# Short output tiles' weights split in own memory, first weights loaded first, and a norm factor moved to a later stage

## The reference, cut to what matters

```python
h = h + mix                                  # mix ends in a product with w_o, 1024 x 1024
hn = rmsnorm(h, norm_ffn[layer])             # (h * rsqrt(mean(h*h) + eps)) * gain
u, gate = jnp.split(hn @ w_in, 2, axis=-1)   # each 2816 wide: 22 tiles of 128
a = conv_b + sum(ext[:, j:j + T] * conv_w[j] for j in range(CONV_W))
h = h + (jax.nn.silu(a) * gate) @ w_out
```

## Time and profile before

| | |
|---|---|
| median of 3 runs | 1583.49 us (1582.51 to 1584.4) |
| the profiled execution, its own time | 1583.71 us |
| its span in the trace | 1582.2 us |
| PE busy | 1535.4 us (97%) |
| DVE, ACT, POOL busy | 977.3, 748.6, 464.3 us |

### The profile page before, as it was taken

One profiled execution on the slowest core, in us unless ns is written; L12 is line 12 of the kernel. 1 busy time (PEld: TensorE's weight loads), 2 busy tenths in 40 slices (PEclk: granted clock), 3 DMA queues, 4 the chain that ended last, 5 costly groups with the idle time before them and its releaser, 6 DMA issues. The chain is left out here.

```text
span 1582.2 us, 36661 instructions
## 1 busy us (share of the span) xinstructions
PE 1535.4 (97%) x13694; PEld 1456.7 (92%) x13694; DVE 977.3 (62%) x1700; ACT 748.6 (47%) x1283; POOL 464.3 (29%) x495
## 2 busy tenths in 40 slices
PE   7999999998999999999999999999999999999997
PEld 7999999988989999999999999755899899999997
DVE  5767666756977777633354444678559776776221
ACT  6444444425456566522244455666444565565110
POOL 1222222213765565101000100223137655551000
PEclk9999999999999999999999999999999999999999
DMA  6222222212232322222333434599422223223230
GB/s 211 69 83 90 90 83 76 77 54 102 81 92 96 103 82 88 93 77 83 91 115 114 138 100 148 182 342 356 139 81 81 90 98 101 85 87 103 91 107 25
DMA packets 52883, 174.14 MB, mean 110 GB/s; under 512 B 7266, under 2 KB 9330, under 8 KB 52770
## 3 DMA queue, kind: packets, MB, share of 16 engines
q1 hardware_dynamic: 47858, 155.46, 30.2%
q0 software_dynamic: 4912, 17.12, 3.0%
HBM read 159.99 MB, written 12.57 MB: 109 GB/s over the span
## 5 line engine op out<-in xcount | busy, mean ns | idle before, releaser
L533 ACT ACTIVATE w_hi<-w_raw 128x1024 fp32r<-128x1024 f32 (+2 forms) x146 | 148.0, 1014 | 299.7 <-PE acc L2025 267.0
L1033 DVE TENSOR_TENSOR w_lo<-w_raw,w_hi 128x1024 fp32r<-128x1024 f32 (+2 forms) x144 | 180.9, 1257 | 141.8 <-ACT w_hi L533 138.9
L2025 PE MATMUL acc<-xl,w_hi 128*128 128x288 f32 x1008 | 228.1, 308 | 14.9 <-DVE w_lo L1238 9.4
L2025 PE MATMUL acc<-xh,w_hi 128*128 128x288 f32 x1008 | 216.7, 297 | 0.0
L2025 PE MATMUL acc<-xh,w_lo 128*128 128x288 f32 x1008 | 216.7, 297 | 0.0
L2025 PEld LDWEIGHTS acc<-xl,w_hi 128*128 128x128 f32 x1008 | 162.8, 190 | 23.0 <-DVE w_lo L1238 9.4
L2217 PE MATMUL aux<-ffn_xsl,w_hi 128*128 128x288 f32 x576 | 169.9, 295 | 3.1 <-issue 2.9
L2217 PE MATMUL aux<-ffn_xsh,w_lo 128*128 128x288 f32 x576 | 170.1, 295 | 0.0
L2217 PE MATMUL aux<-ffn_xsh,w_hi 128*128 128x288 f32 x576 | 169.9, 295 | 0.0
L2025 PEld LDWEIGHTS acc<-xh,w_hi 128*128 128x128 f32 x1008 | 163.1, 190 | 0.0
L2025 PEld LDWEIGHTS acc<-xh,w_lo 128*128 128x128 f32 x1008 | 162.7, 190 | 0.0
(11 more groups left out here) (341 smaller groups left out, 3456.2 us busy)
## 6 DMA issues: line engine op xcount, KB each, us to landing
w_raw<-w_fi_in SPq DMA_DIRECT2D x88, 512.0 KB, 3.7
w_raw<-w_fo_in SPq DMA_DIRECT2D x32, 512.0 KB, 3.6
att_Vd<-cache_v_in SPq DMA_DIRECT2D x32, 512.0 KB, 5.6
w_raw<-w_mix_in SPq DMA_DIRECT2D x31, 512.0 KB, 3.7
w_raw<-w_kv_in SPq DMA_DIRECT2D x16, 512.0 KB, 3.7
w_raw<-w_qg_in SPq DMA_DIRECT2D x16, 512.0 KB, 3.6
dec_Kd<-cache_k_in SPq DMA_DIRECT2D x16, 512.0 KB, 6.7
w_raw<-cache_k_in SPq DMA_DIRECT2D x16, 512.0 KB, 6.9
```

The lines of the kernel that those rows point to most:

```text
L533: nc.scalar.activation((w_hi[:, pos.slot % SPL] if dst is None else dst)[:, 0:width], w_raw[:, pos.slot, 0:width] if raw is None else raw[ ...
L1033: nc.vector.tensor_tensor(low[:, 0:width], w_raw[:, pos.slot, 0:width] if raw is None else raw[:], high[:, 0:width].bitcast(F32), ALU.subt ...
L2025: mm = nc.tensor.matmul(dst[:, hf, 0:HALF], W[:, 128 * (j0 + j):128 * (j0 + j) + 128], x[:, HALF * hf:HALF * hf + HALF], start=(first and ...
```

## The change

- Start: the first half of the first weight block is loaded and split first, then come the gains and the first tile of x; `S0` waits for the last tile of x.
- Output tiles of layer 0: the four short blocks 40 to 43 each get a quarter of `own_hi` and `own_lo`. They are split during tiles 1 and 2, block 44 in tile 2, block 45 after tile 7. `xh` is made ahead of the square (both layers), and from tile 4 on DVE makes the `xl` of a tile after the `add_h` of the next.
- Plain pairs: `sil` is no longer multiplied by `rms`. POOL multiplies `g0` by `rms` instead, in the first four fast pairs, behind its other work there; only `g_hi` at the end waits for it. In pair 3 the low parts of xn come ahead of the weight sums, and these ahead of the convolution's taps.

The core of the diff (renames and declarations left out):

```diff
@@ SP, start
+            sp.dma_start(w_raw[:, 0, 0:512], d["w_mix"][0][:, 0:512]).then_inc(w_half, 16)
+            sp.dma_start(gains[:], d["gains"]).then_inc(ld_table, 16)
             sp.dma_start(h[:, 0, :], d["x"][0]).then_inc(ld_h[0], 16)
-            sp.dma_start(gains[:], d["gains"]).then_inc(ld_table, 16)
...
-            sp.dma_start(w_raw[:, 0, 0:512], d["w_mix"][0][:, 0:512]).then_inc(w_half, 16)
@@ ACT, out_tile and start
-                square(n_s, m)
                 if g is not None:
                     gain_hi(xh, m, g)
+                square(n_s, m)
...
+            act.wait_ge(w_half, 16)
+            nc.scalar.activation(w_hi[:, 0, 0:512], w_raw[:, 0, 0:512], ACT.Copy).then_inc(s_hi, 1)
             act.wait_ge(setup, 1)
@@ ACT, ffn, loop over m
-                    elif m == AHEAD:
-                        hi(Pos(B_REST + 2), W_REST, ready=(block_done, B_WO0 + AHEAD + 1), dst=own_hi)
-                    elif m == AHEAD + 1:
-                        hi(Pos(B_REST + 3), W_REST)
-                        hi(Pos(b_in), ready=(block_done, B_REST + 1))
-                    elif m and m != DT - 2:
-                        hi(Pos(b_in - 8 + m + 2), W_REST if 2 <= m < AHEAD else 1024)
+                    elif m == 0:
+                        hi(Pos(B_REST - 1))
+                    elif m < 3:
+                        for r in (2 * m - 2, 2 * m - 1):
+                            hi(Pos(B_REST + r), W_REST, ready=(block_done, B_WO0 + AHEAD + 1), dst=rest_hi[r])
+                    if layer == 0 and m == 2:
+                        hi(Pos(b_in), ready=(block_done, B_REST - 1))
                     out_tile(m, n_h0 + m + 1, None, s_base + m, G_FFN + 8 * layer)
+                if layer == 0:
+                    hi(Pos(b_in + 1), ready=(block_done, B_REST))
@@ DVE, ffn, loop over m (the lo calls move as the hi calls do)
+                    if layer == 0 and m == AHEAD:
+                        continue
+                    if layer == 0 and m > AHEAD:
+                        gain_lo(xl, xh, m - 1, G_FFN + 8 * layer, x_base + m - 1)
+                        continue
                     gain_lo(xl, xh, m, G_FFN + 8 * layer, x_base + m)
+                if layer == 0:
+                    gain_lo(xl, xh, DT - 1, G_FFN + 8 * layer, x_base + DT - 1)
+                    lo(Pos(b_in + 1))
@@ DVE, plain_pair
-                    taps(k, f)
                     if f == PLAIN - 1:
+                        x_lo_raw(f)
                         weight_sum(0, 0, PLAIN // 2)
                         weight_sum(1, 0, PLAIN // 2)
-                    x_lo_parts(f)
+                        taps(k, f)
+                    else:
+                        taps(k, f)
+                        x_lo_raw(f)
+                    x_lo_sums(f)
                     if f < PLAIN - 1:
                         lo(Pos(b_in + 2 * k + 3, i, 4))
-                    dve.wait_ge(silr_ok, PLAIN * layer + f + 1)
+                    dve.wait_ge(sil_ok, n + 1)
@@ POOL, start, plain_pair, and the end of fast_pair
+            pool.wait_ge(ld_h[DT - 1], 16)
             pool.dma_start(S0[:].rearrange("p n v -> p (n v)"), d["s0"][0]).then_inc(s0_in, 16)
...
-                    pool.wait_ge(sil_ok, n + 1)
-                    nc.gpsimd.tensor_tensor(sil[:], sil[:], rms[:], ALU.mult).then_inc(silr_ok, 1)
...
+                    if isinstance(i, int) and f < 2 * PLAIN:
+                        pool.wait_ge(prod_ok, FT * layer + f - PLAIN + 1)
+                        nc.gpsimd.tensor_tensor(g0[:, f - PLAIN], g0[:, f - PLAIN], rms[:], ALU.mult).then_inc(g_rms, 1)
@@ ACT, g_hi
+                    if f < PLAIN:
+                        act.wait_ge(g_rms, PLAIN * layer + f + 1)
@@ PE, short tiles
-                             split=(own_hi, own_lo) if own else None)
+                             split=(rest_hi[m - AHEAD], rest_lo[m - AHEAD]))
```

More of the change, by code:

```diff
@@ L151, in build @@
         own_hi, own_lo = own_slot("hi", [P, 1024], F32R), own_slot("lo", [P, 1024], F32R)
+        rest_hi, rest_lo = [[t[:, W_REST * r:W_REST * (r + 1)] for r in range(AHEAD)] for t in (own_hi, own_lo)]
         kd0 = fr
@@ L312, in build @@
         s0_in, s0_mul, s1_ps, s1_ok, s1_out, s_out = [sem(n) for n in ("s0_in", "s0_mul", "s1_ps", "s1_ok", "s1_out", "s_out")]
-        st_in, ubuf_ok, u_ok, c0_ok, c2_ok, sil_ok, silr_ok, prod_ok, gh_ok, glo_ok, cst_ok = [sem(n) for n in (
-            "st_in", "ubuf_ok", "u_ok", "c0_ok", "c2_ok", "sil_ok", "silr_ok", "prod_ok", "gh_ok", "glo_ok", "cst_ok")]
+        st_in, ubuf_ok, u_ok, c0_ok, c2_ok, sil_ok, g_rms, prod_ok, gh_ok, glo_ok, cst_ok = [sem(n) for n in (
+            "st_in", "ubuf_ok", "u_ok", "c0_ok", "c2_ok", "sil_ok", "g_rms", "prod_ok", "gh_ok", "glo_ok", "cst_ok")]
         out_cst = sem("out_cst")
@@ L652, in _ @@
                 gain_hi(xh, m, G_MIX)
-                if m == 0:
-                    act.wait_ge(w_half, 16)
-                    nc.scalar.activation(w_hi[:, 0, 0:512], w_raw[:, 0, 0:512], ACT.Copy).then_inc(s_hi, 1)
                 if m == 1:
@@ L1248, in add_square @@
                     nc.vector.tensor_tensor(ssq[:], ssq[:], (rms, sq)[m % 2][:], ALU.add).then_inc(ssq_done, 1)
+            half_lo(0, s_hi, 1, s_lo)
             for m in range(DT):
                 gain_lo(xl, xh, m, G_MIX, m)
-                if m == 0:
-                    half_lo(0, s_hi, 1, s_lo)
                 if m == 1:
@@ L1303, in ffn @@
                         lo(Pos(b_in - 8 + m + 2))
-                    elif m == AHEAD:
-                        lo(Pos(B_REST + 2), W_REST, dst=(own_hi, own_lo))
-                    elif m == AHEAD + 1:
-                        lo(Pos(B_REST + 3), W_REST)
-                        lo(Pos(b_in))
-                    elif m and m != DT - 2:
-                        lo(Pos(b_in - 8 + m + 2), W_REST if 2 <= m < AHEAD else 1024)
+                    elif m == 0:
+                        lo(Pos(B_REST - 1))
+                    elif m < 3:
+                        for r in (2 * m - 2, 2 * m - 1):
+                            lo(Pos(B_REST + r), W_REST, dst=(rest_hi[r], rest_lo[r]))
+                    if layer == 0 and m == 2:
+                        lo(Pos(b_in))
+                    if layer == 0 and m == AHEAD:
[3 more added lines that the diff above has]
+                        continue
                     gain_lo(xl, xh, m, G_FFN + 8 * layer, x_base + m)
+                if layer == 0:
+                    gain_lo(xl, xh, DT - 1, G_FFN + 8 * layer, x_base + DT - 1)
+                    lo(Pos(b_in + 1))
                 dve.wait_ge(rms_done, n_norm + 1)
@@ L1342, in x_scaled, with x_lo_raw @@
                     op.then_inc(xn_ok, 1)
-                def x_lo_parts(j):
+                def x_lo_raw(j):
                     r = DT // 2 * layer + j
@@ L1350, in x_lo_parts, with x_lo_sums @@
                     nc.vector.tensor_tensor(xsl[:, 1:3, j], halves(xn[:, 1]), xsh[:, 1:3, j].bitcast(F32), ALU.subtract).then_inc(s_lo, 1)
+                def x_lo_sums(j):
+                    r = DT // 2 * layer + j
                     dve.wait_ge(s_hi, x_part_n(r) + 3)
@@ L2197, in ffn @@
                         pe.wait_ge(al_ok, DT + 1)
-                    own = layer == 0 and m in (0, AHEAD + 2)
+                    own = layer == 0 and m == 0
                     if layer == 0 and m >= AHEAD:
                         gemm(Pos(b_in - 8 + m), t_in - 8 + m, (t_in + m) % 2, range(AHEAD_K, DT), rh, rl,
-                             split=(own_hi, own_lo) if own else None)
+                             split=(rest_hi[m - AHEAD], rest_lo[m - AHEAD]))
                         continue
```

## The result

| | before | after |
|---|---|---|
| median | 1583.25 us (1582.51 to 1584.4, 4 runs) | 1566.25 us (1565.95 to 1567.13, 4 runs) |
| ratio | | 0.9891, interval 0.9876 to 0.9906 |
| the profiled execution, its span | 1583.71, 1582.2 us | 1566.23, 1564.7 us |

The change gives 17.0 us, where the prediction had 13.7. In another set of runs the same kernel had 1567.65 us (1566.8 to 1568.14) beside 1583.6 before, ratio 0.9897; so 16 to 17 us. Both lie within the predicted range, the first by little: the upper ends of the terms made 16.9, and 17.0 is inside only because the edge was rounded down to 1566.

A forecast was written before the change was run, and what follows sets the result against it. The prediction took PE's list, with work for 97% of the span, as the bound. Its terms 1.5 + 6.1 + 2.5 + 3.6 = 13.7 us gave 1569.8 us, 60 in 100, range 1566 to 1575.5.

The forecast's parts named there:

- Start: First loads and matmul: PE starts at 7.4 instead of 9.36, block 1 limits the gain; 1.5 us, bounds 2.4 and 0.3 later.
- sum of lower ends: Whole kernel: the terms' lower ends, 0.3, 4.5, 1.2 and 2.0, were summed to 8.0 us, giving 1575.5 us.
- Output tiles: Layer 0's short output tiles: PE runs tiles 4 to 7 nearly without a gap; 6.1 us, bounds 4.5 and 6.7.
- Plain pair 0: Both layers: DVE's lo takes 1.22 without POOL's product, PE's wait for the bank goes; 2.5 us, bounds 1.2 and 2.6.
- Plain pair 3: Both layers: DVE ends the pair 1.8 us earlier, so do the third and fourth Strassen products' sums; 3.6 us in all.
- Of this 0.6 counts: End of pair 2: of the 1.22 us saved on DVE's lo, 0.6 counts, as pair 3's u tile was ready at 1221.60.
- The product in the Strassen pairs: POOL's eight moved products, 1.43 to 2.3 us each, are covered by its waits for ACT; 0 us.
- the first: Rival at the start: x comes when the half block did, so no gain there; 1571.6 us, chance 12 in 100.
- second: Rival in the short tiles: half their waits stay as squares and xl meet; 3.1 us less gain, 1572.9, chance 10 in 100.
- fifth: Rival: POOL's queue becomes the bound, delaying product_second and weight splits; up to 18.3 us, 1588.1, chance 6 in 100.
- The fourth: Rival in the Strassen pairs: POOL's eight products each hold DVE up by 1.22; 9.8 us less gain, 1579.6, chance 4 in 100.
- The third: Rival in pair 3: silu ends last, so the pair gives nothing; 3.6 us less gain, 1573.4, chance 8 in 100.

The follow-up runs named there:

- s0_early: The changed kernel with the DMA of S0 issued at once, as before; 1568.02 us, ratio 0.9898 to the kernel before.
- start_only: The kernel before with only the new start; 1582.30 us, ratio 0.999.
- product_only: The kernel before with only POOL's product moved to the Strassen pairs; 1576.22 us, ratio 0.9947.
- order_undone: The changed kernel with DVE's old order in pair 3 (taps, weight sums, low parts of xn); 1567.67 us, ratio 0.9897 to the kernel before.
- triple_product: The changed kernel with POOL's product made three times in each of the eight Strassen pairs; 1573.58 us, ratio 0.9931 to the kernel before.
- order_only: The kernel before with only DVE's new order in pair 3; 1585.67 us, ratio 1.0015.
- snap_early: The changed kernel with ACT's first copy, of the u tile, ahead of three splits at pair 3's end; 1567.51 us, ratio 0.9897 to the kernel before.
- snaps_early: The changed kernel with ACT's first three copies moved ahead of its splits in each layer's first Strassen pair; 1563.98 us, ratio 0.9878 to the kernel before.
- after_again: The changed kernel measured once more, nothing altered; 1567.65 us, ratio 0.9897 to the kernel before.
- tiles_only: The kernel before with only the output tiles' part of the change; 1576.55 us, ratio 0.995.

## Where the prediction was right, and the step that failed

**Start**: forecast 1.5, in the pair of profiles 1.6; x usable at 5.65 (5.6 forecast), first matmul 7.42 (7.4), block 1 the second limit. The mechanism, S0 beside the first loads, is shown by s0_early. That 1.5 and 1.6 agree is in part luck. Block 1's data came at 10.63 where the forecast had 10.0, and PE was only 0.85 us ahead when it began on it (13.00 and 13.85); the rest came back by the 201st matmul. The prediction's sum of lower ends also has a slip: the start's is 0.3 later than now, so -0.3, and the ends make 7.4 and not 8.0. The profiled execution of before had an early start. In the four kernels with the old start the 201st matmul lies at 40.00, 40.65, 40.73 and 41.37 us, in the nine with the new at 37.64 to 38.94, median 38.12; by these medians the start is worth 2.6. start_only gives 1.4 in the median; its profile has lost 0.4 to the lower clock in block 44.

**Output tiles**: forecast 6.1, measured 6.6, inside the bounds. Block 44 ended at 380.7 instead of the forecast 381.2 (382.7 less the start's 1.5), and the low part of block 45 ran partly beside POOL's last sum (1.61 from 380.14) where the forecast put it behind. A detail was wrong: `xl` took 0.82 in the first two short tiles only and 1.41 and 1.42 in the last two. It cost nothing, since by then `add_h` ran ahead of it and PE had no wait behind it. Two small edits inside this term, which the forecast did not price alone, are worth 1.1 (the deferred `xl`) and 1.7 (`xh` ahead of the square).

**Plain pair 0**: forecast 2.5, measured 1.35 + 1.24 = 2.6. The low part at 1.22, no wait for DVEq.

**Plain pair 3**: forecast 1.8 a layer, measured 2.83. This is the term that was mis-sized, and two thirds of the miss of 3.3 us. It is also above the 2.6 a layer that the range was made with, though the prediction's own bound for the pair was 3.65. The step that failed is "Of this 0.6 counts", for the `lo` saved at the end of pair 2, with what is drawn from it, "Together DVE is done with the pair 1.8 earlier". The 0.6 itself came. But the sentence looks only at when DVE comes to the u tile, and puts the rest of what DVE won at nothing. DVE won 1.2 in each of the pairs 0 to 2; it came 0.6 late to the u tile of pair 3 before, and stands 1.62 ahead of it now. So it makes `ffp_xn` of pair 3 earlier by more than the u tile comes earlier, and POOL's four sums of x begin 1.5 ahead of the u tile (419.09 and 420.63) where they began 0.2 behind it (430.99 and 430.83). They run at 0.8 each and are over when DVE comes to its taps. From the u tile's first row to the first low part of a weight sum DVE took 11.09 us before (430.83 to 441.92) and 8.86 after (420.63 to 429.49): 2.23 less, of which 1.23 is the `xsl` that was counted (1.98 to 0.75) and 0.97 the taps that were not (2.67 to 1.70). With the 0.6 this is 2.83. product_only shows 2.75 of it with the old order, so the order is not the cause; order_undone puts its share at 0.1 a layer.

That two such instructions don't share but wait for each other is seen in these rows: 2.67 is 1.70 and 0.97, a little over one POOL sum of 0.81. The Trainium skill (SBUF — State Buffer, Who interferes with whom) adds that the order of issue decides who is held up. The trace agrees: in the kernel before POOL's sums took 1.79 and 1.22 and the taps 2.67. In the one after, POOL's last sum started at 421.52 and kept its 0.82, the low part that started behind it at 421.73 was held up (1.69), and the taps have their plain duration because POOL is done first.

**The product in the Strassen pairs**: forecast 0 with 1.4 to 2.3 us each, followed by a wait for ACT; measured 1.43 to 1.45, and PE's shift does not move in these pairs. The cover was thinner than the two pairs of the earlier trace rows let expect: in the first pair of each layer the wait behind the product was 0.83. triple_product shows that there was room beyond these waits.

**The waits that stay**: the fourth product waits 1.29 for ffn_u as before, as forecast. The third does not wait any more (forecast 1 us): the weight sum is 1.0 earlier than was counted, by the same missed term.

**Whole and parts**: alone the parts measure -7.4, -7.1, -1.4 and +2.0, together -13.9; the whole 16 to 17. Most of the gap is order_only's +2.0, of which 0.8 is the order and the rest goes with a lower clock. With the product moved the order gives 0.2. With -0.2 in place of +2.0 the parts make -16.1. The traces say the same more finely: without the start and the attention the steps of the parts are 8.0 + 6.6 - 0.8 = 13.8 and those of the whole 14.8, and the 1.0 between them is the order, -0.8 alone and +0.2 beside the product.

**The rivals**: the first (start gives nothing), second (half the waits stay) and fifth (POOL's queue) are refuted by the rows above. The fourth's mechanism is there once a layer and no more: the first pair's taps took 2.68 instead of 1.70 beside POOL's product, and PE did not wait for it. The third acts in order_only alone.

## What to carry to other kernels

When a stall on one engine goes, ask also what that engine now finishes earlier for a third one: here POOL's sums moved out from under DVE's taps, which was worth 1.0 us a layer beside the 1.2 of the stall itself. A wait behind an engine's list can hop from one consumer to the next; look at all the instructions that the next consumers wait for before moving one (snap_early against snaps_early). And an order that helps beside one edit can cost without it, so judge such edits in the trace of the combination.

## What the runs showed of the hardware

**The first loads scatter when they run side by side.** With S0's DMA beside SP's loads the first matmul came at 9.36, 10.36, 10.59, 10.75 and 10.25 us in five kernels that load the same bytes (the last one in the new order); without it at 6.88 to 7.91 in nine kernels with the same start. One profile of before therefore under-reads the worth of the start by 1 us.

**The attention stage has two lengths, and TensorE's granted clock makes them.** The stretch of 200 matmuls around 1000 to 1025 us took 24.2 us in five profiles and 25.1 to 25.6 in nine; the same kernel had 24.20 and 25.42. The same 16 matmuls in after and in after_again:

```profile
1004.20 1.92 PE L2420 MATMUL acc<-dec_Kd,dec_Qb 128*32 128x512 f32 x16
```

```profile
1004.31 3.56 PE L2420 MATMUL acc<-dec_Kd,dec_Qb 128*32 128x512 f32 x16
```

In after the granted clock was 1.00 over them, in after_again 0.50 (1004.3 to 1007.6 us), which is the lower of its two levels, 1.2 GHz instead of 2.4. In twelve of the fourteen profiles the clock falls to half somewhere behind a wait of PE for DVE (dec_Pr) of 2.4 us, and what counts is where. In the five short ones it does not fall (tiles_only, snap_early) or is full again 3.7 us behind the end of this wait: at full clock PE has a wait of 1.58 us for ACT there (tiles_only), which takes up what it loses. In the nine long ones it is at half at some time between 5.2 and 8.9 us behind it, where its waits are of 0.34 and 0.35 us only (tiles_only). So 0.9 to 1.4 us of difference in a profile belong to no change, and a pair of profiles should be compared for its clock, stretch by stretch, before a step is given to an edit. A mean clock of 0.997 in both does not show it.
